# Two buffers in turn for the conditioning chunks of the second recurrence, the second one in unused columns of the context tokens

## What is computed

```python
for l in range(DEPTH):
    ctx_out = l < DEPTH - 1
    mod = silu_c @ w_ada[l] + b_ada[l]                # 6 x 1024 shifts, scales, gates
    hx = rmsnorm(x) * (1 + sc_a) + sh_a
    hc = rmsnorm(ctx) * (1 + mc[1]) + mc[0]
    ux = hx @ w_in[l]                                 # 2304 columns
    base_c = 0 if ctx_out else OFF_K
    uc = hc @ (w_in[l] if ctx_out else w_in[l][:, OFF_K:OFF_HQ])
    fx = fourier_mix(...)
    ax, ac = attention_group(...)
    rx, rc = hgrn_group(...)                          # the recurrence, forward and backward
    x = x + g_a * (jnp.concatenate([fx, ax, rx], axis=-1) @ w_out[l])
    x = x + g_f * swiglu(rmsnorm(x) * (1 + sc_f) + sh_f, w_gate[l], w_up[l], w_down[l])
```

## Time and profile before

| | |
|---|---|
| median of 3 runs | 2028.42 us (2027.78 to 2032.68) |
| the profiled execution | 2029.84 us; its span in the trace is 2028.1 us |
| mean granted TensorE clock | 0.923 of full speed |
| busy share of the span | PE 89%, weight loads 80%, VectorE 63%, ScalarE 41%, GpSimd 4% |
| DMA | 300 MB, mean 148 GB/s |
| second recurrence in the trace | from about 973 us to 1078 us |

### The profile page before, as it was taken

The page is one execution under the profiler, slowest core; times in us unless marked ns, Lnnn a source line. Parts: engine busy times, 40 slices in busy tenths (PEclk is TensorE's granted clock), DMA queues, the critical chain, the costliest instruction groups (busy, mean ns, idle before and its releaser), DMA issues.

```text
span 2028.1 us, 31000 instructions
## 1 busy us (share of the span) xinstructions
PE 1804.2 (89%) x12350; PEld 1622.2 (80%) x12350; DVE 1278.6 (63%) x2340; ACT 827.1 (41%) x1589; POOL 85.5 (4%) x153
## 2 busy tenths in 40 slices
PE   4799888989999999798677999968799997889997
PEld 2689767888888888797466999866799977779996
DVE  1335767558877666567566788756578874465544
ACT  2533664142222322435442544346444434555432
POOL 0000232000000000001020000000000000000000
PEclk8899888799999999898679999978899998899999
DMA  8462011045547654232324898632289873415653
GB/s 262 156 200 71 27 43 43 11 136 166 182 158 211 180 182 147 85 102 71 104 85 120 245 277 273 222 94 63 84 261 279 277 228 98 105 42 146 187 177 125
DMA packets 359119, 300.36 MB, mean 148 GB/s; under 512 B 8048, under 2 KB 333408, under 8 KB 358720
## 3 DMA queue, kind: packets, MB, share of 16 engines
q1 hardware_dynamic: 357584, 294.22, 47.5%
q0 software_dynamic: 1392, 4.15, 0.8%
HBM read 297.30 MB, written 1.05 MB: 147 GB/s over the span
## 4 chain that ended last, share of the span: by engine, by line
PE 73%; DVE 12%; DMA 6%; ACT 5%; issue 4%; SPq 0%; DVEq 0%; ACTq 0%; POOLq 0%
PE bank L913 71%; ACT whigh L1452 2%; PE bank L927 2%; DMA raw<-in_ffn_w_in 2%; DVE wlow L1902 2%; DMA AWH<-in_ada_w 1%; DVE ACC L1918 1%; DMA raw<-in_ffn_w_out 1%; DVE A L2206 1%; DVE A L2007 1%; DMA A<-in_w_ada 1%; ACT A L1630 1%; DMA X<-in_ctx 0%; DVE nmax L2175 0%; DVE A L2324 0%
## 5 line engine op out<-in xcount | busy, mean ns | idle before, releaser
L1902 DVE TENSOR_TENSOR wlow<-raw,whigh 128x2048 fp32r<-128x2048 f32 (+1 forms) x183 | 410.1, 2244 | 335.3 <-ACT whigh L1452 334.5
L1452 ACT ACTIVATE whigh<-raw 128x2048 fp32r<-128x2048 f32 (+1 forms) x183 | 343.1, 1878 | 289.2 <-PE bank L913 137.3
L913 PE MATMUL bank<-HTH,whigh 128*128 128x256 f32 (+1 forms) x1424 | 443.5, 311 | 2.1 <-DVE HTL L1995 1.7
L913 PE MATMUL bank<-HTH,wlow 128*128 128x256 f32 (+1 forms) x1424 | 438.8, 308 | 0.0
L913 PE MATMUL bank<-HTL,whigh 128*128 128x256 f32 (+1 forms) x1424 | 438.4, 308 | 0.0
L913 PE MATMUL bank<-whigh,HTH 128*128 128x256 f32 (+1 forms) x1008 | 297.5, 295 | 19.7 <-DVE HTL L2077 6.3
L913 PE MATMUL bank<-wlow,HTH 128*128 128x256 f32 (+1 forms) x1008 | 292.7, 290 | 0.0
L913 PE MATMUL bank<-whigh,HTL 128*128 128x256 f32 (+1 forms) x1008 | 292.5, 290 | 0.0
L913 PEld LDWEIGHTS bank<-HTH,whigh 128*128 128x128 f32 x1424 | 271.6, 191 | 15.6 <-DVE HTL L1995 2.5
L913 PEld LDWEIGHTS bank<-HTH,wlow 128*128 128x128 f32 x1424 | 271.6, 191 | 13.6
L913 PEld LDWEIGHTS bank<-HTL,whigh 128*128 128x128 f32 x1424 | 271.7, 191 | 12.7
(11 more groups left out here) (210 smaller groups left out, 2337.6 us busy)
## 6 DMA issues: line engine op xcount, KB each, us to landing
raw<-in_ffn_w_in SPq DMA_DIRECT2D x88, 512.0 KB, 5.3
A<-in_ada_w SPq DMA_DIRECT2D x38, 1024.0 KB, 6.7
A<-in_w_ada SPq DMA_DIRECT2D x32, 1024.0 KB, 5.4
raw<-in_w_gate SPq DMA_DIRECT2D x44, 512.0 KB, 5.1
raw<-in_w_up SPq DMA_DIRECT2D x44, 512.0 KB, 6.4
raw<-in_ffn_w_out SPq DMA_DIRECT2D x20, 1024.0 KB, 5.0
raw<-in_w_in SPq DMA_DIRECT2D x18, 1024.0 KB, 5.6
raw<-in_w_down SPq DMA_DIRECT2D x18, 1024.0 KB, 5.1
```

Source lines behind the costliest of these rows:

```text
L913: return nc.tensor.matmul(out, lhsT, rhs, start=start, stop=stop, skip_group_check=True)
L1452: nc.scalar.activation(parts(loads[n])[0], raw_slot(loads[n]), ACT.Copy).then_inc(*made("split_high", loads[n]))
L1902: V.tensor_tensor(low, raw_slot(loads[n]), as_float(high), ALU.subtract).then_inc(*made("split_low", loads[n]))
```

## The change

`ada_place` gives the chunks of layer 1's recurrence the slots 1 and 7 in turn. So c0, c2, c4, c6, c8 stay in `AWH`, and c1, c3, c5, c7, c9 go to the new slot 7: columns 0 to 767 and 1792 to 2047 of tiles 2 and 3 of `U`, four parts k of 256 columns in each tile. The load of a chunk now waits for the use of the chunk two before it. A load into slot 7 is four DMAs (384 KB and 128 KB for each of the two tiles) where one DMA of 1 MB stood. `ada_part` gives TensorE the 256 columns of a part. The spots, the arithmetic and the order of everything else stay. The key 1 in the diff is the group of the scan spots of layer 1; layer 0's recurrence keeps one slot.

```diff
             group = ada_group(ada_spot[l, j])
             members = [c for c in ada_chunks if ada_group(ada_spot[c]) == group]
-            slots = {"start": (0, 1, 2, 3), "projection": (5, 6), "feed_forward": (2, 3, 4)}.get(group[0], (1,))
+            slots = {"start": (0, 1, 2, 3), "projection": (5, 6), "feed_forward": (2, 3, 4), 1: (1, 7)}.get(group[0], (1,))
             n = members.index((l, j))
             slot = slots[n % len(slots)]
-            where = AWH[:, slot] if slot < 2 else AWX[slot - 2] if slot < 5 else AWU[slot - 5]
+            where = AWH[:, slot] if slot < 2 else AWX[slot - 2] if slot < 5 else AWU[slot - 5] if slot < 7 else None
             return slot, where, members[n - len(slots)] if n >= len(slots) else None
 
         def ada_part(w, k):
 
+            if w is None:
+                a = (0, 256, 512, OFF_HQ)[k % 4]
+                return U[:, 2 + k // 4, a:a + 256]
             return w[:, k, :] if len(w.shape) == 3 else w[:, k // 4, k % 4, :]
...
                 if slot < 5:
                     sp.dma_start(dst, src).then_inc(*made(f"ada_weights{slot}", l, j, by=16))
+                elif slot == 7:
+                    for half in range(2):
+                        for a, k, n in ((0, 0, 3), (OFF_HQ, 3, 1)):
+                            sp.dma_start(U[:, 2 + half, a:a + 256 * n].rearrange("p (k c) -> p k c", k=n),
+                                         src[:, 4 * half + k:4 * half + k + n]).then_inc(*made(f"ada_weights{slot}", l, j, by=16))
                 else:
```

## The result

The changed kernel took 2002.8 us, the median of 3 runs (1999.52 to 2006.48), against 2028.42 us before: a ratio of 0.9868, 95% interval 0.9831 to 0.9905. Two later comparisons of the same two kernels gave 0.9896 (0.9878 to 0.9915) and 0.9877 (0.9852 to 0.9903).

The account below looks back on a forecast made before the run. TensorE was taken to bound the kernel (73% of the chain that ended last). Waits of 15.5 us plus 1.5 us of clock made 17.0 us, so the median of 2028.42 would become 2011.4 us, range 2005 to 2019.

Parts of the forecast that it names:

- c1's and c6's waits of 5.49 us: Second recurrence: TensorE's waits for the loads of c1 and c6 vanish, a gain of 5.49 us each.
- The cover of the gates of steps 3 and 4: Second recurrence: gates from ScalarE and VectorE still arrive before TensorE needs them, by 0.8 and 0.5 us.
- the sum of the waits, 15.5 us: Second recurrence: gains ahead of c1, c2, c3 and c6 of 5.49 + 2.35 + 2.15 + 5.49 us.
- It waits about 0.3 us: Ahead of c2: TensorE's wait for the load shrinks from 2.65 to about 0.3 us, a gain of 2.35.
- c6's 5.49 and c1's 5.49 have no gate in them: Said against the rival of nothing measurable: these two waits hide no wait for gates, so at least 11 us come.
- the term for the clock, 1.5 us: Gain from an earlier 2.4 GHz grant, about half of the 3.3 us at 1039 to 1046; bounds 4 us loss, 10 gain.
- The two terms of the upper bound: Clock's upper bound of 10 us: 3.3 us from work at 1039 to 1046, half of 7.9 us at 1026 to 1034.
- rival B: Without holes the granted clock stays at 1.00 from about step 4: 23.5 us gained, 2004.9 us; chance 0.14.
- A: Slot 7's four DMAs pay fixed costs in series, so c3 and c1 are late: 8.7 us gained, 2019.7; chance 0.10.
- C: Nothing measurable: gates, not loads, set the pace, or the change doesn't do what it says; 2025 to 2028 us; chance 0.05.
- D: Slower: the granted clock falls to half from 1046 to 1078, up to 27 us added, 2040.1 us; chance 0.03.
- The estimate of 1.6 us ahead of c3: Lateness of c3 if slot 7's four DMAs take 10.4 us in series; the waits' sum would be 13.9 us.

Follow-up runs that it names:

- only_c6: The kernel before with only chunk c6 in slot 7, each other load waiting as before: ratio 0.9964 (0.9949 to 0.9979) to the kernel before, 7.3 us shorter.
- before_filled: The kernel before, one buffer, with 62 idle matmuls ahead of the waits for c1, c2, c3 and c6: 2026.2 against 2033.4 us, ratio 0.9961.
- before_again: The kernel before, unchanged, measured again against the kernel before: ratio 0.9997 (0.9978 to 1.0017).
- only_c1: The kernel before with only chunk c1 in slot 7, each later load waiting for the chunk just ahead: ratio 0.9967 (0.9948 to 0.9987), 6.7 us shorter.

## Why the prediction was right or wrong

**Right: the waits for loads and their places.** c1's and c6's waits of 5.49 us for the load went whole. c3's went, its load was in time, four issues and all. The 7.5 us of added issues on SyncE's queue cost nothing. The cover of the gates of steps 3 and 4 was thin and held. Outside the second recurrence nothing moved that the unchanged kernel doesn't move too. In the trace the forecast for the stretch was 101.56 - 17.0 = 84.6 us, and three traces gave 81.2 to 82.4.

**Wrong: the sum of the waits, 15.5 us.** "It waits about 0.3 us" ahead of c2: it waited 3.9, 1.0 and 4.1 us in three traces. I had let TensorE reach c2 at the pace of before. In the first and third trace the clock was up behind c0, and it got there 10.6 and 10.5 us after the start of the stretch instead of 13.1; in the second it was not up, and it got there after 12.9. c2 itself began 14.5, 13.9 and 14.6 us after the start, against the 13.4 of the forecast: the load set that time, and it took 5.9 to 6.6 us from its issue to c2, where I had taken 5.3.

And "c6's 5.49 and c1's 5.49 have no gate in them" was wrong for c6. The hole ahead of c6 had hidden a wait for the gates: with it gone TensorE stands 1.7 us for LFL ahead of `prepare(6)` in all three traces (0.35 us in `only_c6`), so c6's term was worth 3.8 us there and not 5.49. The waits for loads fell by 12.4 us in the means, from 15.4 to 3.0; less the new wait of 1.7 that is 10.7 of the 11.0 us by which the idle time fell.

**Wrong: the term for the clock, 1.5 us, and this is the step that failed.** The busy time fell by 11.3 us in the means for the same instructions (78.8 to 67.5), 5 to 10 us against the one trace I had (75.1 to 69.9, 67.6, 65.0). I had counted only half of the work right behind the wait for c6. 8.3 of the 11.3 us came in steps 4 and 5: both traces of before have the low clock from the sums of `prepare(5)` through c6 and beyond, and none of the three after has; the levels of step 4 went from 6.24 us to 3.34. The two terms of the upper bound that lie there, 3.3 us and half of 7.9, named the place, and in size rival B (23.5 us, 2004.9) was what happened; it had 0.14. `before_filled` shows the reason that the forecast lacked: with each load still waiting for the chunk ahead of it, the clock is worth some 8 us. Which hole holds the clock down where is not shown. Against B I held that the slow stretch began before the hole at 1034. It had three other holes ahead of it, but they don't settle the matter: between them and the slow stretch the clock was at 1.00, and `only_c6` has all three and 3.39 us in step 4.

**Wrong: the base.** The sum was set against one execution. Its total was typical, but its second recurrence was one of the shorter (101.6; the next trace gave 106.6) and its first one of the longer. The last part of the recurrence, behind step 5's levels, took 28.8 us in that trace and 35.9 in the next. A gain that is read off stretches whose length changes by 5 us from one execution to the next needs a range that is wider than the bounds of its terms.

**The rivals.** A (late split load, 0.10) is out: two, four and eight DMAs take the same. C did not come. D's time did not come either, but what it named did in part: from 1037 to 1055 us TensorE was busy for 16.65 us at 0.54 in the first trace after, and the second is like it. The kernel before does the same in `before_again`, where the levels of step 7 took 6.24 us against 3.34 in its first trace, so the change is not shown to cause it. The rule on the clock that was weighed there, activity releases the slow clock (the Trainium skill, TensorE: Matmul & The Clock Gate, "What's actually happening"), put the gain near the upper bound, and `before_filled` agrees with it (granted clock 0.85 with the holes filled, 0.61 and 0.68 without); the busy slow stretch that I held against it (7.93 of 8 us at 0.50) is real too, so the rule gives the direction and not the moment. The estimate of 1.6 us ahead of c3 rested on the fixed cost in the Trainium skill (DMA: Bandwidth & Descriptors, "Anatomy of one DMA"), taken four times in series. That section gives it for DMAs issued by GpSimd, and these are issued by SyncE. No trace has a wait ahead of c3. The preference for 1 MiB and more in one DMA (the Trainium skill, DMA: Bandwidth & Descriptors, "Rules for kernel authors") shows nowhere in this stretch either: two, four and eight DMAs for 1 MB differ by no more than the traces of one kernel do.

## What to carry to other kernels

A wait of TensorE in a sparse stretch costs its length, less any wait that it hid (1.7 us here), and a slower clock besides: here 11 us less idle time came with 11 us less busy time for the same work. Price both, and take the upper bound of the clock seriously where several holes follow each other. Read the size from several traces: with no edit, this stretch of the kernel before took 101.6 and 106.6 us. A second buffer can lie in columns that a later stage leaves unused, and cutting its load into pieces cost nothing in the traces where the pieces were sent well ahead.

## What was not expected of the hardware

The granted clock differs between executions of one program in the same stretch. The first recurrence, the same code in all kernels, took about 105.1 to 105.8 us (clock 0.80 to 0.81) in six of fourteen traces, 110.1 to 110.8 us (0.74) in six, and 107.9 us (0.78) in two. The kernel before ranged from 2016.8 to 2037.9 us in 12 runs.

Idle matmuls ahead of a wait for a load paid: 62 of them, some 9 us of work that no one reads, made the kernel 8 us shorter. Eight each in gaps under 2 us did not.

Four 1 MB loads, one of them cut in four, all sent within 7.4 us, left the stretch as if there were no loads (77.80 and 77.80 us).

A load of 1 MB into `AWH` was in use 5.3 to 5.5 us after its issue ahead of c1, c2 and c3 before; ahead of c2 in the changed kernel it was 5.9 to 6.6 us, and in `only_c1`, where nothing is queued behind it, 6.5. What makes the difference is not shown.
